# A two-block transformer kernel: the first attention's sums over later keys as two rounded products

## What is computed

```python
z = jnp.einsum("bqhd,bkhd->bhqk", q_blk, k).astype(jnp.float32) * scale
mask = k_pos[None, :] < q_pos[:, None]
neg_log_one_minus_beta = jnp.where(mask, jax.nn.softplus(z), 0.0)
between = lax.cumsum(neg_log_one_minus_beta, axis=3, reverse=True) - neg_log_one_minus_beta
log_a = jax.nn.log_sigmoid(z) - between
a = jnp.where(mask, jnp.exp(log_a), 0.0)
return jnp.einsum("bhqk,bkhd->bqhd", a.astype(v.dtype), v)
```

## Time and profile before

| | us |
|---|---|
| median of 3 runs | 2409.2 (2403.49 to 2417.78) |
| profiled execution | 2407.05 |
| its span, first to last instruction | 2405.2 |
| TensorE busy | 2351.6 (98%) |
| DVE, ACT, POOL busy | 1694.5, 1284.1, 570.6 |
| mean granted clock of TensorE | 0.994 of full |

### The profile page before, as it was taken

The page is one execution under the profiler, slowest core; times in us unless marked ns, Lnnn a source line. Parts: engine busy times, 40 slices in busy tenths (PEclk is TensorE's granted clock), DMA queues, the critical chain, the costliest instruction groups (busy, mean ns, idle before and its releaser), DMA issues.

```text
span 2405.2 us, 42199 instructions
## 1 busy us (share of the span) xinstructions
PE 2351.6 (98%) x16475; PEld 2098.7 (87%) x16475; DVE 1694.5 (70%) x3088; ACT 1284.1 (53%) x2780; POOL 570.6 (24%) x434
## 2 busy tenths in 40 slices
PE   8998999999999999999999999999999999999997
PEld 7878989997899889999888888789989999888886
DVE  5745354446789778887776556869888888777556
ACT  6543345456555665455555555655665455555554
POOL 3626235555379000000000003368300000000000
PEclk9999999999999999999999999999999999999999
DMA  5311155554245556556776564245556655777664
GB/s 192 115 62 55 45 179 180 185 184 147 79 153 183 185 184 196 196 195 207 240 248 217 192 215 150 80 158 175 182 187 192 197 194 190 244 243 238 193 201 140
DMA packets 148086, 420.99 MB, mean 175 GB/s; under 512 B 15920, under 2 KB 49072, under 8 KB 147504
## 3 DMA queue, kind: packets, MB, share of 16 engines
q1 hardware_dynamic: 144080, 405.34, 52.1%
q0 software_dynamic: 2192, 8.99, 1.0%
q10 hardware_dynamic: 1616, 3.96, 0.4%
HBM read 400.40 MB, written 17.83 MB: 174 GB/s over the span
## 4 chain that ended last, share of the span: by engine, by line
PE 93%; DVE 3%; ACT 2%; DMA 1%; issue 0%; POOL 0%; ACTq 0%; DVEq 0%; SPq 0%
PE pb L462 92%; PE pb L471 1%; ACT arena L1234 1%; DVE arena L1754 0%; DVE arena L1751 0%; ACT arena L1422 0%; DMA cst<-in_consts 0%; DMA raw<-in_vT 0%; ACT hi L1222 0%; DMA raw<-in_w_out 0%; DVE sm L2086 0%; DVE H L1751 0%; ACT HT L1520 0%; DVE arena L1902 0%; DVE arena L2218 0%
## 5 line engine op out<-in xcount | busy, mean ns | idle before, releaser
L462 PE MATMUL pb<-HT,hi 128*128 128x256 f32 (+2 forms) x5232 | 1093.8, 302 | 2.5 <-POOL lo L2502 1.9
L1222 ACT CAST hi<-raw 128x512 fp32r<-128x512 f32 x1402 | 817.4, 619 | 373.7 <-PE pb L462 203.0
L462 PEld LDWEIGHTS pb<-HT,hi 128*128 128x128 f32 x5232 | 840.1, 191 | 41.6 <-issue 2.8
L462 PE MATMUL pb<-HT,lo 128*128 128x256 f32 (+1 forms) x2968 | 839.7, 283 | 0.0
L2502 POOL TENSOR_TENSOR lo<-raw,hi 128x512 fp32r<-128x512 f32 x384 | 525.7, 1392 | 465.2 <-ACT hi L1222 464.9
L1761 DVE TENSOR_TENSOR lo<-raw,hi 128x1024 fp32r<-128x1024 f32 x464 | 567.0, 1222 | 41.4 <-ACT hi L1222 41.2
L462 PEld LDWEIGHTS pb<-HT,lo 128*128 128x128 f32 x2968 | 567.2, 191 | 0.0
L462 PE MATMUL pb<-hi,WH 128*128 128x512 f32 x1112 | 433.3, 390 | 0.9 <-DVE WL L2439 0.9
L462 PE MATMUL pb<-lo,WH 128*128 128x512 f32 x1112 | 432.9, 389 | 0.0
L462 PE MATMUL pb<-hi,WL 128*128 128x512 f32 x1112 | 432.7, 389 | 0.0
L2509 POOL DMA_DIRECT2D arena<-in_ln_g x4 | 2.2, 562 | 1263.1 <-PE pb L462 1263.1
(11 more groups left out here) (200 smaller groups left out, 1999.5 us busy)
## 6 DMA issues: line engine op xcount, KB each, us to landing
raw<-in_uT SPq DMA_DIRECT2D x256, 512.0 KB, 3.6
raw<-in_vT SPq DMA_DIRECT2D x256, 512.0 KB, 3.8
raw<-in_w_ffn_in SPq DMA_DIRECT2D x44, 512.0 KB, 3.8
raw<-in_wq SPq DMA_DIRECT2D x32, 512.0 KB, 3.5
wk<-kept SPq DMA_DIRECT2D x128, 128.0 KB, 3.8
raw<-in_w_in SPq DMA_DIRECT2D x24, 512.0 KB, 3.8
raw<-in_w_ffn_out SPq DMA_DIRECT2D x22, 512.0 KB, 4.3
raw<-in_w_gate SPq DMA_DIRECT2D x16, 512.0 KB, 3.2
```

Of the source, the lines that this page charges most:

```text
L462: return e.matmul(o, l, r, start=start, stop=stop)
L1222: e.copy(u.hi[k], u.half[k]).then_inc(*s.up("hi", ("hi", g)))
```

## The change

The sums' moving operand, the softplus values of a head, is split like a weight: ACT rounds it into a high half (`att_hi`), DVE subtracts for the low half (`att_lo`), and `att_c` of TensorE multiplies both by a rounded triangle and rounded ones (both exact), which ACT writes once into `WH` (`SUMS`). The triangle now meets all 400 columns in one instruction. The halves lie in the ring of half-slots: four units named `stick`, without a load and without a raw slot, stand in the stream behind gate 1, two heads to a unit, so that head h's half may be written when the `part` six halves back is announced: v tile 3 for heads 0 and 1, gate 0 for 2 and 3, gate 1 for 4 and 5, heads 0 and 1 themselves for 6 and 7. `take("stick", i)` on ACT moves the splits of gates 2 and 3 behind the fourth and the sixth exponential.

```diff
--- before.py
+++ after.py
@@ -157,7 +157,11 @@
     for n in "qkv":
         for f in range(4):
             add((n, f), d["w_" + n][f], low=pool)
-    for g in range(16):
+    for g in range(2):
+        add(("gate", g), d["w_gate"][g], low=pool)
+    for i in range(4):
+        add(("stick", i), None, cut=False)
+    for g in range(2, 16):
         add(("gate", g), d["w_gate"][g], low=pool)
     for name, g in SIDES:
         add((name, g), d["w_" + name][g], cut=False)
@@ -209,12 +213,12 @@
 
 
 class Unit:
-    def __init__(self, m, i, name, src, cut, dims, low, g):
+    def __init__(self, m, i, r, name, src, cut, dims, low, g):
         self.i, self.name, self.src, self.cut = i, name, src, cut
-        o = (i % RAW) * UN
+        o = (r % RAW) * UN
         self.raw = m.raw[:, o:o + UN]
         self.slot = self.raw.rearrange("p (k n) -> p k n", k=dims) if dims else self.raw
-        self.slot_key = f"raw{i % RAW}"
+        self.slot_key = f"raw{r % RAW}"
         self.g = (g, g + 1)
         self.low = low
         o = (g % PARTS) * HU
@@ -244,10 +248,12 @@
         arena, H, sm = T["arena"], T["H"], T["sm"]
         self.arena, self.H, self.sm, self.wk, self.cst, self.pk, self.bcs = arena, H, sm, T["wk"], T["cst"], T["pk"], T["bcs"]
         self.units = []
-        g = 0
+        g = r = 0
         for i, (name, src, cut, dims, low) in enumerate(stream(d)):
-            self.units.append(Unit(self, i, name, src, cut, dims, low, g))
-            g += 2 if cut else 0
+            self.units.append(Unit(self, i, r, name, src, cut, dims, low, g))
+            g += 2 if cut or name[0] == "stick" else 0
+            r += 0 if name[0] == "stick" else 1
+        self.sticks = [u for u in self.units if u.name[0] == "stick"]
         ar = self.ar
         self.Hv = H[:, :].rearrange("p (t n) -> p t n", t=2)
         self.out = out.rearrange("b (t p) n -> p (b t) n", p=128)
@@ -293,6 +299,7 @@
 
         self.XN = ar(0, 2048).rearrange("p (t n) -> p t n", t=2)
         self.SG = [ar(2048 + i * 256, 256) for i in range(2)]
+        self.SUMS = T["WH"][:, 0:256]
         self.AC = [[T[n][:, i * 256:(i + 1) * 256] for n in ("WH", "WL")] for i in range(2)]
         self.TY = [ar(30000 + i * 256, 256) for i in range(2)]
         self.ST6 = sm[:, 72:96].rearrange("p (t k s) -> p t k s", t=2, k=2)
@@ -597,18 +604,21 @@
         for k in (h, h + 1):
             free[Z_BANK[k]] = [("zm", k)]
 
-    def att_c(h):
-        b = 3 + h % 3
-        s0, s1, s2 = m.SPb[h][:, 0:256], m.SPb[h][:, 256:400], m.SPb[h][0:16, 400:416]
-        tri, ones = m.C("tri"), m.C("ones")
+    def att_c(u, h):
+        b, g, parts = 3 + h % 3, u.g[h % 2], u.part(h % 2)
+        tri, ones = m.SUMS[:, 0:128], m.SUMS[:, 128:256]
         emptied(b)
-        w.wait_ge(*s.to("zs", h))
-        mm(PB[b][:, 0:256], tri, s0, True, False)
-        mm(PB[b][:, 112:256], ones, s1, False, False)
-        mm(PB[b][:, 240:256], ones[0:16, :], s2, False, True)
-        mm(PB[b][:, 256:400], tri, s1, True, False)
-        mm(PB[b][:, 384:400], ones[0:16, :], s2, False, True)
-        mm(PB[b][0:16, 400:416], tri[0:16, 0:16], s2, True, True).then_inc(*s.up("att_ps", ("c_ps", h)))
+        w.wait_ge(*s.to("sums"))
+        w.wait_ge(*s.to("lo", g))
+        for i, v in enumerate(parts):
+            mm(PB[b][:, 0:400], tri, v[:, 0:400], i == 0, False)
+        for v in parts:
+            mm(PB[b][:, 112:256], ones, v[:, 256:400], False, False)
+        for i, v in enumerate(parts):
+            mm(PB[b][0:16, 400:416], tri[0:16, 0:16], v[0:16, 400:416], False, False)
+            mm(PB[b][:, 240:256], ones[0:16, :], v[0:16, 400:416], False, False)
+            x = mm(PB[b][:, 384:400], ones[0:16, :], v[0:16, 400:416], False, i == 1)
+        x.then_inc(*s.up("part", ("part", g), ("c_ps", h)))
         free[b] = [("c2", h)]
 
     def att_y(h):
@@ -642,7 +652,9 @@
     gate()
     gate()
     for h in range(8):
-        att_c(h)
+        if h % 2 == 0:
+            u = units.take("stick", h // 2)
+        att_c(u, h)
         if h > 2:
             att_y(h - 3)
     for h in (5, 6, 7):
@@ -1356,6 +1368,15 @@
         w.wait_ge(*s.to("c2", h))
         fn(m.ZM[h][0:16, 400:416], m.ZM[h][0:16, 400:416], ACT.Exp).then_inc(*s.up("sticks", ("p2", h)))
 
+    def att_hi(h):
+        u, k = m.sticks[h // 2], h % 2
+        w.wait_ge(*s.to("zs", h))
+        w.wait_ge(*s.to("part", u.g[k] - PARTS))
+        e.copy(u.hi[k][:, 0:416], m.SPb[h]).then_inc(*s.up("hi", ("hi", u.g[k])))
+
+    w.wait_ge(*s.to("const"))
+    e.copy(m.SUMS[:, 0:128], m.C("tri")).then_inc(*s.up("sums_in"))
+    e.copy(m.SUMS[:, 128:256], m.C("ones")).then_inc(*s.up("sums_in", ("sums",)))
     for h in range(4):
         att_e(h)
     take("v", 0)
@@ -1383,10 +1404,22 @@
 
     for h in range(8):
         att_l(h)
+        if h in (1, 2):
+            att_hi(h - 1)
     gate()
+    att_hi(2)
+    att_hi(3)
     gate()
+    att_hi(4)
+    att_hi(5)
+    take("stick", 0)
+    take("stick", 1)
     for h in range(8):
         att_p(h)
+        if h < 2:
+            att_hi(h + 6)
+        elif h in (3, 5):
+            take("stick", 2 + h // 5)
     w.wait_ge(*s.to("ga_raw", RAW_GATES - 1))
     raw = m.GA[:, 0:RAW_GATES, :]
     fn(raw, raw, ACT.Sigmoid).then_inc(*s.up("gates", ("ga_first",)))
@@ -1883,15 +1916,23 @@
         tt(m.ZM[h][:, 0:400], m.ZM[h][:, 0:400], PB[b][:, 0:400], S).then_inc(*up("logits", ("c1", h)))
         tt(m.ZM[h][0:16, 400:416], m.ZM[h][0:16, 400:416], PB[b][0:16, 400:416], S).then_inc(*up("logits", ("c2", h)))
 
+    def att_lo(h):
+        u, k = m.sticks[h // 2], h % 2
+        w.wait_ge(*s.to("hi", u.g[k]))
+        tt(u.lo[k][:, 0:416], m.SPb[h], u.hi[k][:, 0:416].bitcast(F32), S).then_inc(*s.up("lo_dve", ("lo", u.g[k])))
+
     for h in range(8):
         att_z(h)
-    for h in range(4):
+    for h in range(8):
         att_s(h)
-    for h in range(4):
-        att_s(h + 4)
+        if h in (2, 3):
+            att_lo(h - 2)
+    att_lo(2)
+    att_lo(3)
+    for h in range(8):
         att_c(h)
-    for h in range(4, 8):
-        att_c(h)
+        if h < 4:
+            att_lo(h + 4)
 
 
     def masked(name, i, dst, banks, nm):
@@ -1971,6 +2012,9 @@
 
     for g in range(16):
         take("gate", g)
+        if g == 1:
+            for i in range(4):
+                take("stick", i)
     for b in (4, 5):
         cs = slice(512 * (b - 4), 512 * (b - 4) + 512)
         w.wait_ge(*s.to("mean_ps", b))
@@ -2606,9 +2653,10 @@
         w.wait_ge(*(s.to("gated", l, 64, q - 4) if q > 3 else s.to("g_ps", l, 63)))
         e.dma_start(m.GL[q % 4], m.kept[l, q]).then_inc(*s.up(f"returned{q % 4}", ("returned", l, q), by=16))
 
-    for i, u in enumerate(m.units):
+    loaded = [u for u in m.units if u.name[0] != "stick"]
+    for i, u in enumerate(loaded):
         if i >= RAW:
-            before = m.units[i - RAW]
+            before = loaded[i - RAW]
             if before.cut:
                 w.wait_ge(*s.to("lo", before.g[0]))
                 w.wait_ge(*s.to("lo", before.g[1]))
@@ -2617,7 +2665,7 @@
                 w.wait_ge(*s.to("side_ps", g, 1 if name == "rwo" else 0, 1))
         elif i:
             w.wait_ge(*s.to("x", 1))
-        e.dma_start(u.slot, u.src).then_inc(*s.up(u.slot_key, ("raw", i), by=16))
+        e.dma_start(u.slot, u.src).then_inc(*s.up(u.slot_key, ("raw", u.i), by=16))
         if u.name[0] in ("u", "v") and len(u.name) == 3:
             l = u.name[1]
             n = u.name[2] + (128 if u.name[0] == "v" else 0)
```

## The result

The change is slower: 2413.02 us against 2408.84 (medians of 20 runs each), ratio 1.0023, interval 1.0015 to 1.0030, where 2403.9 and a gain were forecast; it lies above the forecast's range, which ended at 2412. The profiled execution took 2413.00, 5.95 more than that of before.

What follows compares the result with a forecast made beforehand. TensorE's own stream was taken to bound the kernel: 10.2 us saved on sums less 3.4 idle gives 6.8, less 1.5 for one clock fall, so 2409.2 - 5.3 = 2403.9 us, range 2397.5 to 2412.

Steps and rivals of the forecast that it cites:

- What bounds the kernel: Whole kernel: TensorE, busy 98% of the span and 93% of the last chain; the attention's tail takes 26.6 us without idling.
- The term of the sums: TensorE's sums over later keys: a head's c takes 0.82 us instead of 2.09, eight save 10.2 us.
- the end of 1.05: Upper end of the forecast for a head's sums c: 1.05 us, half of the old c, saving 8.3.
- The waits: TensorE in the attention's tail idles 3.4 us in five pieces, the longest 1.78 ahead of c2, leaving 6.8 saved.
- The layout of ACT and DVE: Queues of rounding copies (0.46 us each) and low halves (0.52 each) among logarithms, sums and exponentials, 0.04 between engines.
- the forecast's own base: Median of the three runs before, 2409.2 us, from which the forecast's gain was subtracted.
- The clock: TensorE's idles in the attention's tail drop the granted clock to 0.50 once, for 3.4 us, costing 1.5 us.
- the forecast of -5.3: Net effect on the kernel: 6.8 us saved less 1.5 for the clock's fall.
- the clock would not fall at all: Rival for the attention's tail: idles too short to lower the clock, giving 2402.4 us; chance 0.2.
- The rival on the slower side: DVE's low halves become the bound in the attention's tail and the time grows, 2414 at 2.25 each; chance 0.04.
- narrow pieces don't run in one pass: Rival for the sums: 144- and 16-column products keep their old time, c about 1.8, giving 2407.8 us; chance 0.1.
- The rest: Behind and beside the tail: GpSimd idle during low halves, gate 2's product with 12 us of cover, half-slots in time; no cost.

Runs made afterwards that it cites:

- e3_nowait: Kernel before, with the sums as single-pass products of a constant, so nothing is split or waited for: 2408.31 against 2406.30, ratio 1.0010.
- e6_only2: Changed kernel plus a burst of 9 bf16 products ahead of head 2's sums only: 2401.28 against 2407.76 for the kernel before, ratio 0.9973.
- e5_only0: Changed kernel plus a burst of 7 bf16 products ahead of head 0's sums only: 2411.34 against 2407.76 for the kernel before, ratio 1.0016.
- e2_fp32: Changed kernel with the sums back in plain fp32, added ACT and DVE work and waits kept: 2408.61 against 2406.30 for the kernel before.
- e7_back: Changed kernel with the sums of heads 4 to 7 in plain fp32, low halves still made: 2417.26 against 2407.76 for the kernel before.
- e8_best: Changed kernel, halves of heads 2 and 3 earlier, 16-column products joined, bursts of 7, 4, 4 ahead of c0, c2, y0: 2402.48 against 2407.76 before.
- e11_stall: Kernel before, fp32 sums, with TensorE holding c2 and c3 back for the previous head's exponential: 2416.81 against 2405.76, ratio 1.0052.
- e9_best2: Changed kernel, halves of heads 2 and 3 earlier, 16-column products joined, bursts of 7, 9, 4 ahead of c0, c2, y0: 2400.51 against 2405.76 before.

## Why the prediction was wrong

*What bounds the kernel* was right: TensorE's stream, and the stretch is where the kernel got slower (+7.2 in the profiles). The profiled executions differ by 5.95, since gate 1 ended 2.9 earlier (it moves by 4 us between these profiles) and what stands behind y7 took 1.7 more. The medians differ by 4.2; what the other 3 us of the stretch went into is not resolved.

*The term of the sums* was mis-sized. c is 1.3, not 0.82, and outside the end of 1.05. The four wide products were nearly as estimated: 0.25, 0.18, 0.07 and 0.07 in the rows after 133.41, 0.57 for 0.50. The six short ones cost 0.72, from 133.98 (133.91 + 0.07) to 134.70, not 0.32. I had taken a step of 0.053 from a row whose products move 128 columns; the pieces with 16 columns on 128 weight columns step 0.11. I read that as the next weight load standing in the open, which the trace does not prove. The trace of before held the better row: in c0 the fp32 records of 16 columns on 128 weight columns, which start at 136.17 and 136.30 with the next record at 136.49, step 0.13 and 0.19. Saved at the upper clock: 8 x (2.09 - 1.3) = 6.3, not 10.2.

*The waits.* The layout of ACT and DVE held, the wait ahead of c2 was over-sized. c0 waited 0.88 (0.80 forecast). The wait ahead of c2 was 0.9 (1.78), since c0 and c1 took longer while lo2 came on time: DVE made lo2 and lo3 at 136.19, 3.7 behind gate 1's end, against 3.8 in my layout, and the first exponential came 5.8 behind it, against 6.0. Idle in all 1.8 instead of 3.4. With these two the change would have gained 6.3 - 1.8 = 4.5 us at the upper clock, or 2404.7 by the forecast's own base of 2409.2.

*The clock* is the step that failed: "One such fall over c3, y0, c4 and y1 costs ... 1.5 us. I expect one." There was one, beginning at c2 (c3 forecast), but of 27.3 us, not 3.4. Its price by the rows: c2 to c7 at 2.30 for 1.3 are 6.0, y0 to y5 at 1.85 for 1.03 are 4.9, the two bursts 0.8: 11.7. 4.5 - 11.7 = -7.2, the measured stretch. Against the forecast of -5.3, the stretch came out 12.5 us worse: 3.9 by the sums, 10.2 by the fall, less 1.6 by the waits. I took the length of a fall from a row behind which dense products stood, without asking whether the products here could end it. The longer fall that I had quoted myself, 183.5 to 190.2, was the warning: short products and idles stood behind that one until 186.87. And an earlier row of before should have told me that idling is not needed:

```profile
88.00:91.20 3.20, 3.20 (x12) 1.54 (x11) 3.17 (x4) 3.20 (x8) 3.20 (x2) 1.00 0.16 29
91.30:94.70 3.40, 3.40 (x16) 3.40 (x17) 3.40 (x3) 1.41 (x5) 3.40 (x3) 0.50 0.29 112
```

From 86.2 to 91.1 TensorE ran sixteen records of plain fp32 without an idle that the profile shows, and the clock fell behind them. In that fall it ran projections without a gap, and the fall ended after 3.4 us.

*The rivals.* That the clock would not fall at all, and the Trainium skill's reason for it (TensorE: Matmul & The Clock Gate, HAM oscillation: idle gaps longer than these), is refuted: e3_nowait fell with 0.49 idle, and the kernel before fell at 91.3 with none ahead of it. The same page's table of the two states has sustained activity release the throttle; here it did not while TensorE was busy for 26.58 of 27.20. The rival on the slower side named DVE; DVE kept to the layout, and the loss came by another way. That narrow pieces don't run in one pass is wrong for those of 144 columns (0.07 each, its price was 0.24); its c of 1.8 is as far above the measured 1.3 as my 0.82 is below.

*The rest* held: GpSimd idle through the low halves, gate 2's product without a wait (5.98 behind y7's end, 5.97 before), the half-slots never short.

## What to carry to other kernels

When products on TensorE get cheaper, read the granted clock of the stretch, and don't only ask whether a wait appears: in e3_nowait cheaper sums dropped it with one idle of 0.49 us. Price a fall by what stands behind it, up to the next dense stretch, and not by the shortest fall in the trace. One burst of 9 full-width bf16 products in the middle of the thin run (e6_only2) turned a ratio of 1.0023 into 0.9973, each against the kernel before on its own chip; a burst of 7 in the wait at its start (e5_only0, 1.0016) was worth next to nothing. And look at the single times beside a profile: in e2_fp32, e7_back and e8_best the profiled execution is one of those with the shorter times, and longer ones with a lower mean clock stand beside it.

## What the runs showed of the hardware

The level of the granted clock can outlast what brought it about. The same alternation of sums and y products, without a burst among them, ran for 12 us at 1.00 in e6_only2 (142.3 to 154.3) and for 21 at 0.50 in the change (139.2 to 159.9), in both cases with TensorE busy throughout. Falls in this stretch lasted 3.4, 13.5, 17, 20, 24 and 27 us. Plain fp32 sums with their y ended a fall without a burst after 17 us (e11_stall), and 13 us after they began in e7_back; the single-pass ones did not before the bf16 bursts came.

A 16-column product on 128 weight columns steps 0.11 at the upper clock: a half's short pieces take 0.26 in threes (134.12 to 134.38 above) and 0.15 where two are joined into one (134.18 to 134.33 in e9_best2). Products of 128 columns on as many weight columns step 0.053; why the shorter ones step more was not tested. Nor was it told apart which property of these products lets the clock fall or keeps it down.
